# Pairs of a routed block in a ring of eight, and a residual that is loaded ahead with the shared expert's rows added by DMA

## What is computed

```python
x = layer_norm(DEEPNORM_ALPHA * x + mix, ln1_g, ln1_b)              # x1
scores = sigmoid(xt @ w_router)                                     # 64 experts
_, idx = top_k(scores + router_bias, 8)
gates = sel / sum(sel) * 2.5                                        # sel: the 8 scores
routed = sum over the 8 experts of gate * (silu(xb @ w_gate[e]) * (xb @ w_up[e])) @ w_down[e]
shared = swiglu(xt, w_gate_sh, w_up_sh, w_down_sh)                  # one expert for all tokens
x = layer_norm(DEEPNORM_ALPHA * x + routed + shared, ln2_g, ln2_b)  # ALPHA = 2 ** 0.25
```

## Time and profile before

| | |
|---|---|
| median of 3 runs | 1599.1 us (1592.4 to 1612.2) |
| profiled execution | 1605.3 us, of which its span (first to last instruction) 1603.7 |
| TensorE busy | 1414.9 us, 88% of the span |
| VectorE, ACT, POOL busy | 66%, 48%, 33% |
| DMA | 357 MB, 223 GB/s over the span |
| by stage | to x1: 471 us; item loop: to about 1480; tail: 124 us |

### The profile page before, as it was taken

How to read it: one execution, slowest core, us unless ns; L and a number is a source line. 1 busy time by engine, 2 the same in 40 slices (tenths; PEclk the granted TensorE clock), 3 DMA queues, 4 the chain that set the end, 5 groups by cost and what they waited for, 6 DMA issues and landing times.

```text
span 1603.7 us, 26837 instructions
## 1 busy us (share of the span) xinstructions
PE 1414.9 (88%) x6543; PEld 1140.1 (71%) x6544; DVE 1053.4 (66%) x1188; ACT 773.5 (48%) x1056; POOL 534.2 (33%) x455
## 2 busy tenths in 40 slices
PE   6966947799969999999998999999999989997874
PEld 5865636577758887878877888888878767786331
DVE  4399857277774495865776456666777776483677
ACT  3121155221143485765676456566766776474000
POOL 1057010136642243434443243344343433341000
PEclk9988977798879999999999999999999999999987
DMA  5112040121264596967888577677797897593995
GB/s 200 53 40 79 0 157 26 79 79 49 58 224 158 184 344 264 360 238 248 314 320 321 208 238 274 246 282 292 264 365 257 311 360 282 216 333 111 425 422 231
DMA packets 93455, 357.34 MB, mean 223 GB/s; under 512 B 36864, under 2 KB 36992, under 8 KB 64880
## 3 DMA queue, kind: packets, MB, share of 16 engines
q1 hardware_dynamic: 42512, 276.22, 46.0%
q0 software_dynamic: 34928, 74.32, 12.6%
q10 hardware_dynamic: 15984, 6.40, 1.5%
HBM read 327.25 MB, written 63.15 MB: 243 GB/s over the span
## 4 chain that ended last, share of the span: by engine, by line
PE 60%; DMA 16%; DVE 13%; issue 6%; ACT 2%; ACTq 1%; POOL 0%; SPq 0%; POOLq 0%; DVEq 0%
PE ps L1517 28%; PE ps L1535 12%; DMA xg<-x_d,idx 7%; PE ps L1335 6%; DVE cv L956 4%; PE ps L1360 4%; DMA ydx<-list_d 2%; PE ps L1449 2%; DMA idx<-list_d 2%; DMA xsh<-y_d 2%; PE ps L1601 1%; DMA yg<-y_d 1%; PE ps L1553 1%; DVE whl L913 1%; PE ps L1407 1%
## 5 line engine op out<-in xcount | busy, mean ns | idle before, releaser
L1517 PE MATMUL ps<-wgu,xTe 128*128 (+1 forms) x2496 | 599.9, 396 | 12.5 <-issue 10.6
L1517 PEld LDWEIGHTS ps<-wgu,xTe 128*128 128x128 f32 x2496 | 465.3, 190 | 110.1 <-issue 17.1
L1215 DVE TENSOR_TENSOR wgu<-raw,wgu (+1 forms) x130 | 292.1, 2289 | 10.0 <-issue 9.8
L582 POOL DMA_INDIRECT y_d<-ysb,ydx x99 | 136.8, 1382 | 485.4 <-DMA ydx<-list_d 267.2
L1535 PE MATMUL ps<-wdn,hT 128*128 (+1 forms) x1236 | 297.2, 389 | 0.0
L1535 PEld LDWEIGHTS ps<-wdn,hT 128*128 128x128 f32 x1236 | 232.0, 188 | 48.1
L746 ACT CAST wgu<-raw (+1 forms) x130 | 249.6, 1921 | 1.1 <-SPq L398 0.5
L1220 DVE TENSOR_TENSOR xTe<-ps,xTe 128x512 fp32r<-128x512 f32 x210 | 134.9, 684 | 141.1 <-ACT xTe L799 135.2
L575 POOL DMA_INDIRECT xg<-x_d,idx x97 | 170.6, 1759 | 110.8 <-PE ps L1335 54.6
L1215 DVE TENSOR_TENSOR wdn<-raw,wdn (+1 forms) x65 | 149.0, 2292 | 46.1 <-ACT wdn L792 39.9
L804 ACT COPY ysb<-ps 128x512 f32<-128x512 f32 x204 | 109.5, 589 | 121.1 <-PE ps L1535 113.0
(11 more groups left out here) (208 smaller groups left out, 1246.7 us busy)
## 6 DMA issues: line engine op xcount, KB each, us to landing
raw<-in_w_gate SPq DMA_DIRECT2D x64, 1024.0 KB
raw<-in_w_up SPq DMA_DIRECT2D x64, 1024.0 KB
raw<-in_w_down SPq DMA_DIRECT2D x64, 1024.0 KB
yg<-y_d SPq DMA_DIRECT2D x16, 1536.0 KB, 19.4
yg<-y_d SPq DMA_DIRECT2D x8, 1024.0 KB, 24.5
wraw<-in_w_in SPq DMA_DIRECT2D x10, 512.0 KB, 3.3
xin<-in_x POOLq DMA_DIRECT2D x8, 512.0 KB, 4.8
wraw<-in_w_kv SPq DMA_DIRECT2D x8, 512.0 KB, 3.3
```

What stands on the lines that cost most here:

```text
L582: g.indirect_dma_start(out=y_d, out_offset=bass.IndirectOffsetOnAxis(ap=ydx[:, s, 1:2], axis=0), in_=ysb[:, s], in_offset=None, bounds_che ...
L1215: V.tensor_tensor(dst, raw_, hi.bitcast(F), ALU.subtract).then_inc(done, 1)
L1517: last = mm(ps[:, 2 + s, :], xTe[:, s, st, d], wgu[:, w, mo, d].rearrange("p a n -> p (a n)"), start=(d == 0 and st == 0 and mo == 0), sto ...
```

## The change

Five things change, all between x1 and the end.

1. `idx` gets eight slots (RING) instead of two, and `ydx` with all its loads goes: POOL loads an item's pairs once, three items ahead, the gather takes the token number from the slot and the put the row number. The slot is taken again once the put of the item five before has landed.
2. SP writes each x1 tile twice, to `x1_d` and to `xa_d`. All eight tiles of the shared expert's rows go out through POOL as DMAs that add to `xa_d` (`add_shared`), after ACT has scaled them by 1/ALPHA. ACT stores nothing for them, and waits for these DMAs where it waited for its own.
3. So the residual of the tail is `xa` = x1 + shared/ALPHA, and the gates are divided by ALPHA too, as is EPS by ALPHA squared; the LayerNorm's result is the same. `xa` (4 MB) is loaded in two DMAs where before `token_rows` of tiles 0 and 1 (2 MB) stood.
4. TensorE adds `xa` and four expert rows (PEK) instead of two other rows and three; VectorE adds four. The chunks are rows 0 to 3, 4 and 5, 6 and 7. ACT makes 32 scaled identities instead of 25.
5. In the tail VectorE ends the statistics of tile t before it normalises tile t-1.

POOL's loop is now written out over eight items, without conditions up to item 71.

```diff
-BYHAND = 4
-PEK = 3
+RING = 8
+ALWAYS = (NT + E) // RING
+PEK = 4
...
                 sp.wait_ge(s_x1, t + 1)
-                sp.dma_start(x1_d[t * 128:(t + 1) * 128, :], xres[:, t % 2]).then_inc(s_x1w[t % 2], 16)
+                for rows in (x1_d, xa_d):
+                    sp.dma_start(rows[t * 128:(t + 1) * 128, :], xres[:, t % 2]).then_inc(s_x1w[t % 2], 16)
...
-                    sp.wait_ge(s_x1w[t % 2], 16 * (t // 2 + 1))
+                    sp.wait_ge(s_x1w[t % 2], 32 * (t // 2 + 1))
...
             for s in range(2):
-                sp.wait_ge(s_ysh[s], 16 * BYHAND // 2)
-                token_rows(s)
+                sp.wait_ge(s_yd[s], 16 * NT // 2)
+            for n in range(2):
+                sp.dma_start(xa[:, 4 * n:4 * n + 4],
+                             xa_d[n * 512:(n + 1) * 512, :].rearrange("(t p) d -> p t d", p=128)).then_inc(s_xa[n], 16)
             sp.wait_ge(s_endR, 4)
             for t in range(NT):
...
                 expert_rows(t)
-                if t >= 1 and t + 1 < NT:
-                    sp.wait_ge(s_pc, t)
-                    token_rows(t + 1)
...
+            def add_shared(j):
+
+                g.wait_ge(s_y, 2 * j + 4)
+                g.dma_start(xa_d[j * 128:(j + 1) * 128, :], ysb[:, j % 2], accum_op=ALU.add).then_inc(s_yd[j % 2], 16)
+
+            add_shared(0)
+            add_shared(1)
...
+            def load_pairs(q, c):
+                lb = g.value_load(tab[0:1, 2, bass.ds(q * RING + c, 1)], min_val=0, max_val=LIST - 128)
+                g.dma_start(idx[:, c % RING], list_d[bass.ds(lb, 128), :]).then_inc(s_idx[c % RING], 16)
...
+            def put_rows(q, c):
+
+                g.wait_ge(s_idx[c % RING], 16 * nth_use(q, c))
+                g.wait_ge(s_y, 2 * (q * RING + c) + 4)
+                g.sem_inc(s_seen, 1)
                 g.indirect_dma_start(
-                    out=y_d, out_offset=bass.IndirectOffsetOnAxis(ap=ydx[:, s, 1:2], axis=0),
-                    in_=ysb[:, s], in_offset=None,
-                    bounds_check=SHARED + S - 1, oob_is_err=False).then_inc(s_yd[s], 16)
...
+                    out=y_d, out_offset=bass.IndirectOffsetOnAxis(ap=idx[:, c % RING, 1:2], axis=0),
+                    in_=ysb[:, c % 2], in_offset=None,
+                    bounds_check=S * K - 1, oob_is_err=False).then_inc(s_yd[c % 2], 16)
+
+            def fetch(q, c):
+
+                gather(q, c + 1)
+                g.wait_ge(s_yd[(c - 5) % 2], 16 * nth_put(q, c - 5))
                 g.sem_inc(s_seen, 1)
...
+                load_pairs(q, c + 3)
+                if isinstance(q, int) and q * RING + c - 3 < NT:
+                    add_shared(q * RING + c - 3)
+                else:
+                    put_rows(q, c - 3)
+
+            for j in range(3):
+                load_pairs(1, j)
+            add_shared(2)
+            add_shared(3)
+            gather(1, 0)
+            add_shared(4)
+            for r in range(RING):
+                fetch(1, r)
+            with g.Fori(2, ALWAYS) as q:
+                for r in range(RING):
+                    fetch(q, r)
...
-            def y_out(slot):
+            def y_out(slot, scale):
                 for b in range(2):
-                    nc.scalar.copy(ysb[:, slot, b * 512:(b + 1) * 512], ps[:, 5 + b, :]).then_inc(s_y, 1)
+                    nc.scalar.activation(ysb[:, slot, b * 512:(b + 1) * 512], ps[:, 5 + b, :], ACT.Copy,
+                                         scale=scale).then_inc(s_y, 1)
...
-                    if not shared:
+                    if not known or i >= 4:
                         act.wait_ge(s_yd[s], 16 * nth)
-                        lb = act.value_load(tab[0:1, 2, bass.ds(i - 2, 1)], min_val=0, max_val=LIST - 128)
-                        act.dma_start(ydx[:, s], list_d[bass.ds(lb, 128), :]).then_inc(s_ydx[s], 16)
                     act.wait_ge(s_dn, i - 1)
-                    y_out(s)
+                    y_out(s, 1.0 / ALPHA if known else 1.0)
...
-                pe.wait_ge(s_cl[t % 2], 32 * (t // 2 + 1))
+                pe.wait_ge(s_xa[t // 4], 16)
                 for h in range(2):
-                    cols = slice(h * 512, (h + 1) * 512)
-                    mm(ps[:, 2 * r + h, :], adiag[:], x1c[:, t % 2, cols], start=True, stop=False)
-                    mm(ps[:, 2 * r + h, :], ident[:], xsh[:, t % 2, cols], start=False, stop=False)
+                    mm(ps[:, 2 * r + h, :], ident[:], xa[:, t, h * 512:(h + 1) * 512], start=True, stop=False)
```

More of the change, by code:

```diff
@@ L124, in build @@
         ysb = at("ysb", 176, [128, 2, D])
-        idx = at("idx", 184, [128, 2, 2], U32)
-        ydx = at("ydx", 184.25, [128, 2, 2], U32)
+        idx = at("idx", 184, [128, RING, 2], U32)
         cmp_ = at("cmp_", 192, [128, 2, NE])
@@ L133, in build @@
         yg = at("yg", 0, [128, 4, K, D])
-        x1c = at("x1c", 128, [128, 2, D])
-        xsh = at("xsh", 136, [128, 2, D])
-        acc = at("acc", 144, [128, 3, D])
+        xa = at("xa", 128, [128, NT, D])
+        acc = [at("acc0", 176, [128, D]), at("acc1", 180, [128, D]), at("acc2", 197, [128, D])]
         diag = at("diag", 160, [128, NT, PEK, 128])
-        adiag = at("adiag", 172, [128, 128])
         g2 = at("g2", 189, [128, D])
@@ L264, in build @@
         s_xs = (sem("s_xs0"), sem("s_xs1"))
-        s_idx = (sem("s_idx0"), sem("s_idx1"))
+        s_idx = [sem(f"s_idx{r}") for r in range(RING)]
         s_xg = (sem("s_xg0"), sem("s_xg1"))
@@ L420, in _ @@
             sp.sem_inc(s_dready, 1)
-            def token_rows(t):
-                r = slice(t * 128, (t + 1) * 128)
-                sp.dma_start(x1c[:, t % 2], x1_d[r, :]).then_inc(s_cl[t % 2], 16)
-                sp.dma_start(xsh[:, t % 2], y_d[SHARED + t * 128:SHARED + (t + 1) * 128, :]).then_inc(s_cl[t % 2], 16)
             def expert_rows(t):
@@ L564, in _, with nth_use @@
             n_items = g.value_load(nit[0:1, 0:1], min_val=NT + E, max_val=MAX_ITEMS)
-            def token_list(i, s):
-                lb = g.value_load(tab[0:1, 2, bass.ds(i, 1)], min_val=0, max_val=LIST - 128)
-                return lambda: g.dma_start(idx[:, s], list_d[bass.ds(lb, 128), :]).then_inc(s_idx[s], 16)
-            def gather(i, s, nth):
-                g.wait_ge(s_idx[s], 16 * nth)
-                g.wait_ge(s_et, i - 1)
+            def nth_use(q, c):
+                return q + c // RING
@@ L604, in _ @@
-            gather(NT, 0, 1)
-            put_item(NT - 4, 0, 1)
-            with g.Fori(0, GROUPS) as group:
-                with g.If(n_items > 2 * GROUP * group + NT - 1):
-                    with g.Fori(0, GROUP) as pair:
-                        jj = GROUP * group + pair
-                        with g.If(n_items > 2 * jj + NT - 1):
-                            fetch(2 * jj + NT, 0, jj + 1, jj + 1)
-                            put_item(2 * jj + NT - 3, 1, jj + 1)
-                            with g.If(n_items > 2 * jj + NT):
-                                fetch(2 * jj + NT + 1, 1, jj + 2, jj + 1)
-                                put_item(2 * jj + NT - 2, 0, jj + 2)
@@ new lines, in _ @@
+            gather(1, 0)
[5 more added lines that the diff above has]
+                    fetch(q, r)
+            with g.Fori(ALWAYS, (MAX_ITEMS + 2) // RING + 1) as q:
+                with ExitStack() as inner:
+                    for r in range(RING):
+                        inner.enter_context(g.If(n_items > RING * q + r - 3))
+                        fetch(q, r)
@@ L628, in _ @@
+            past = g.value_load(nit[0:1, 1:2], min_val=E, max_val=MAX_ITEMS - NT)
+            for s in range(2):
+                g.wait_ge(s_xg[s], 16 * ((past + 5 - s) // 2))
+                g.wait_ge(s_yd[s], 16 * ((past + 9 - s) // 2))
             g.sem_inc(s_endR, 1)
             for t in range(NT):
-                rstd(NT + 2 + t)
+                g.wait_ge(s_pv, NT + 2 + t)
+                g.tensor_tensor(rs[:, t % 2:t % 2 + 1], mv[:, t % 2, 1:2], neghalf[:, 0:1], ALU.pow).then_inc(s_pw, 1)
@@ L826, in step_act @@
                     act.wait_ge(s_gu, i)
-                if shared and 2 <= i < 2 + BYHAND:
-                    act.wait_ge(s_y, 2 * i)
-                    act.dma_start(y_d[SHARED + (i - 2) * 128:SHARED + (i - 1) * 128, :], ysb[:, s]).then_inc(s_ysh[s], 16)
-                elif shared and i >= 2:
-                    act.dma_start(ydx[:, s], list_d[(i - 2) * 128:(i - 1) * 128, :]).then_inc(s_ydx[s], 16)
                 if shared:
@@ L885, in _ @@
             act.wait_ge(s_endR, 4)
-            nc.scalar.activation(adiag[:], ident[:], ACT.Copy, scale=ALPHA).then_inc(s_dg, 1)
             for t in range(NT):
@@ L1120, in route @@
                 settle()
[L1121 removed]
+                step(V.tensor_scalar(gates[:, u], sel[:], gs[:, 1:2], ROUTED / ALPHA, ALU.mult, ALU.mult))
             v.wait_ge(s_wrhi, 1)
```

119 lines of the change are left out of this document (43 added, 76 removed).

## The result

| | before | after |
|---|---|---|
| median | 1602.2 us (4 runs, 1592.4 to 1612.2) | 1545.2 us (4 runs, 1543.0 to 1547.6) |
| profiled execution, its span | 1605.3, 1603.7 | 1544.5, 1542.9 |
| TensorE busy, share of the span | 1414.9, 88% | 1395.5, 90% |
| GpSimd's gathers, 97 and 99 | 170.6 us | 102.7 us |

The ratio is 0.9617, 95% interval 0.9577 to 0.9658: the change makes the kernel 3.8% faster. The forecast was 1558 us.

The account below looks back on a forecast made before the run. Bounds: TensorE, stalled by late gathers in the item loop; DMA bytes in the tail. Span 1603.7 - 32 (loop) + 1.5 (shared stage) - 2 (loop end) - 15 (tail) = 1556.2, plus 1.6 around it: 1558 us, range 1541 to 1583.

Parts of the forecast that it names:

- rival F: Whole kernel: no remainder, no stall in the shared stage, no clock fall in the tail; 1546 us, chance 0.10.
- forecast A: Whole kernel: the forecast itself, 1558 us, ranging alone from 1550 to 1568; chance 0.58.
- Late gathers hang on the ydx wait: Item loop: POOL's put waits for the 1 KB ydx load, delaying the gather behind it; about 41 us.
- The remainder of 9 us in the item loop: Item loop: 9 of 41 us stay, 2 for each of four or five full runs; so -32 us, from -41 to -10.
- The case worked out in the prediction: Item loop, one step: with an early put, rows come at 598.3 to 600.4, and TensorE needed them at 602.4.
- The phase of puts and gathers: Item loop: puts and gathers move but stay in reach of VectorE's weight subtractions; a gather keeps POOL 1.02 to 3.10 us.
- The shared stage at +1.5: Shared stage: step 4's copy of y may wait for the first accumulating DMA; cost 0 to 7 us, taken as +1.5.
- D: Shared stage: eight slow accumulating DMAs, T long each, pace seven steps; 1583 us at T = 13 us; chance 0.08.
- End of the loop, -2: End of the item loop: the last put, held by the ydx load before, goes at 1474.4 instead of 1476.37; -2 us.
- The tail, -15: Tail: bound by bytes, which fall from 44.1 to 37.7 MB; -15 us, from -17 to -8.
- C: Tail: TensorE stays at its lower clock level, 17 us a tile; kernel 1602 us, chance 0.04.
- B: Item loop: DMA bounds runs of one-block experts, weights come late; loop gives 10 us instead of 32; 1580 us, chance 0.20.

Follow-up runs that it names:

- no_lock: Kernel before, with VectorE's expert-step weight subtractions reading their second input as zeros from PSUM instead of SBUF; 1588.6 us against 1602.0.
- ring_no_lock: Changed kernel, with VectorE's expert-step weight subtractions reading their second input as zeros from PSUM; 1543.7 us against 1543.4.
- idx_late: Changed kernel, but pairs are loaded two items ahead and only after the gather of the item before has landed; 1552.3 us.
- pek3: Changed kernel, but in the tail TensorE sums three expert rows of a tile and VectorE five; 1545.1 us.
- more_512: Changed kernel, with 512 KB more loaded from HBM for each of 60 experts into SBUF that nobody reads; 1557.5 us.
- ydx_back: Changed kernel, but each expert item's put takes its rows from a separate list again, loaded by ScalarE two steps later; 1583.0 us.
- ydx_early: Changed kernel with a separate list for the puts, which ScalarE starts loading at the end of the step before the copy of y; 1587.5 us.
- plain_add: Changed kernel, but the eight shared row tiles are written over the copy of x1 by plain DMAs, without the addition; 1545.8 us.

## What held of the forecast, and the step that failed

In the way the forecast was made, before's span was to lose 47.5 us; it lost 60.8. The direction, the range and the mechanisms held; three of its four terms were too cautious. What came is nearly rival F (1546 us, chance 0.10), and not forecast A. F's condition on the clock was not met, though: the last tile began at the lower level in half of the profiles.

**Late gathers hang on the ydx wait.** Right, and now shown: put back alone, it costs 38 us; with the wait taken away or the load started early, nothing. Two of the prediction's signs are there: no list waits of GpSimd that count, and TensorE's waits for gathers at 0. The third was set too tight: puts start 0.9 us behind the copy, and not under half a microsecond.

**The remainder of 9 us in the item loop** is the step that failed. The loop was to lose 32 us and the shared stage to cost 1.5; together they gave 39.8. Of the 13.3 us that the sum was short, 7.8 are this term. Behind the shared tiles (from step 8 on) the 43.0 us of excess became 2.7, so 40.4 went where 32 were forecast. Two numbers were mis-sized. The 41 us of late gathers were 43.0: the "some 3 us" put down to the shared tiles are mostly this wait of the kernel before, which ends ahead of step 1 (471.99), and these tiles had 1.3 in the steps counted:

```profile
470.93 1.09 PE L1335 MATMUL ps<-ident,xg 128*128 128x128 f32 x8 [3.46 <-DMA xg<-x_d]
```

And the remainder was 2.7 instead of 9, of which 2.4 lie at steps 87, 89 and 94. At the first two ScalarE comes late to weights (timeline of the changed kernel); what held the third the trace doesn't name:

```profile
1267.19 1.91 ACT L742 CAST wgu<-raw  x1 [2.20 <-SPq L392]
...
1271.53 5.72 PE L1499 MATMUL ps<-wgu,xTe 128*128 x24 [0.38 <-ACT wgu L742]
```

I gave each of four or five full stretches 2 us of stall, on the ground that DMA was nearly full there and only 2 to 4 us were in hand. The stretches are as full as I thought, 376 to 391 GB/s, and the 2 to 4 us in hand were right, but they are enough: counted from the start of its issue, a gather lies 14.4 us ahead of its use in the median (13.5 at least), and the slowest of the late ones took 11.8. None was late. The case worked out in the prediction already gave a remainder of none; the margin of the sum didn't come from it but from caution.

**The phase of puts and gathers.** "Not out of reach" of VectorE's subtraction is right for the puts, 1.6 us beside it, and wrong for the gathers: none of 99 took more than 1.09 us. They stand behind the put, which is the one held until the subtraction ends. That the row beat the page was right (no_lock); what it meant for the sum was not, as ring_no_lock shows: 0 us.

**The shared stage at +1.5** cost at most 0.6 (excess of steps 1 to 7: 1.8, before 1.3). The first two accumulating DMAs issue from 492.26, 3 us before the prediction's 495.2, and the copy that needs the first waits until 498.46: it landed within 6.2 us of its issue, between the bounds of 2.6 and 11.8. The earlier start was luck, as nothing in the forecast asked for it; from 495.2 the copy would have come at 501.4, 2.1 us after it was wanted and still within the 4 us held to be free. Two traces of the experiments have landings of these DMAs: 6.7 to 8.9 us in idx_late and 5.2 to 11.5 in pek3. The 11.5 is past a step of 9.29 and delayed nothing, as such a DMA has two steps. D, with a T of 13 us or more, didn't come.

**End of the loop, -2:** -1.9.

**The tail, -15:** -17.5. The terms: the last tile's first rows 82.1 us after the first load instead of 83.5 (426 to 429 GB/s instead of 424, and less start); the last store 1542.9 - 1539.8 = 3.1 us instead of 4.3; the fall of the clock in the last tile, +1.5 in the sum, costs 1.8 where it happens, which is in half of the profiles. The 1.5 us up to step 1 were not forecast and mean nothing: step 1 starts between 469.9 and 477.1 in the sixteen profiles. C, a clock that stays low, didn't come: the level rose within each tile. The Trainium skill (TensorE: Matmul & The Clock Gate, "HAM oscillation — how this bites in real kernels") describes a kernel cold on every tile; here the 16 records took over 8.7 us on the first, the fifth and the last tile of eight.

**B:** weights came late, but with 6.3 us of waits in sum and under 3 us of time. By more_512, 31.5 MB more would have made it a case of 12 us.

Open: which tiles fall to the lower clock. In the profiles of the ten kernels with this tail, idle times ahead of the 16 records were 2.24 to 3.13 us where a tile behind the first fell and up to 3.19 where none did (none fell at 1.93 or less), so the idle time alone doesn't tell.

## What to carry to other kernels

Of a queue that waits, ask whether it waits for its input or for something small that was requested late; a 1 KB load can take 6 to 8 us to land beside large transfers, so start it by its latency, not by its size. Loading it one depth earlier was worth 38 us here, and leaving one load out nothing. Where two causes of lateness stand in series, remove the one that waits and check the other before working on it: it may no longer cost anything. And when a case worked out in full gives no remainder, don't add one for fullness alone; look at how much time lies ahead of the use.

## What the runs showed of the hardware that was not expected

- The issue of an indirect DMA on GpSimd (1.0 us) takes up to 3.1 us when it starts while a VectorE operation with two SBUF inputs runs, and ends 0.9 us after it (before and after, 142 issues). It is not held when it has begun before the operation (36 gathers of after), nor when one input comes from PSUM, for the same 2.28 us of VectorE time (no_lock).
- A list load of 1 KB lands in 1.7 us at the least, where the DMA share around it is under 0.3, and in 7.1 to 7.7 in the median where it is over 0.9 (ydx_back, ydx_early, no_lock, ScalarE's loads). Over a whole run the medians are 5.8 to 6.5 us for ScalarE's loads and 5.5 to 8.9 for GpSimd's.
- A DMA of 512 KB that adds to DRAM holds GpSimd's queue 0.92 us in place of 0.55 (plain_add). It landed within 6.2 us with two under way, and in 5.2 to 11.5 us in pek3 and idx_late.
- 512 KB more of weights per expert took 9.0 us to land in the median, and the loop absorbed five sixths of their transfer time (more_512).
